# Gated MLP on one core: spatial products in blocks of four feature tiles between the two halves of each down projection

## The reference

```
z = gelu(hn @ w_in)                 # 1024 -> 4096
u, v = split(z, 2)                  # 2048 each
v = layernorm(v, g, b)
sv = W_s v + b_s                    # per block of 128 tokens and group of 256 columns; W_s is 128 x 128, masked
h = h + (u * sv) @ w_out            # 2048 -> 1024
```

## Time and profile before

| | |
|---|---|
| time, median of 3 runs | 2132.33 us (2126.59, 2132.33, 2132.35) |
| profiled execution, its own time | 2127.57 us |
| its span | 2125.8 us |
| TensorE weight loads (PEld) busy | 1689.2 us (79%) |
| VectorE (DVE) busy | 1220.3 us (57%) |
| ScalarE (ACT) busy | 756.9 us (36%) |
| GpSimd (POOL) busy | 194.0 us (9%) |

### The profile page before, as it was taken

How to read it: one execution, slowest core, us unless ns; L and a number is a source line. 1 busy time by engine, 2 the same in 40 slices (tenths; PEclk the granted TensorE clock), 3 DMA queues, 4 the chain that set the end, 5 groups by cost and what they waited for, 6 DMA issues and landing times.

```text
span 2125.8 us, 24372 instructions
## 1 busy us (share of the span) xinstructions
PE 2045.3 (96%) x10045; PEld 1689.2 (79%) x10045; DVE 1220.3 (57%) x1795; ACT 756.9 (36%) x1187; POOL 194.0 (9%) x96
## 2 busy tenths in 40 slices
PE   6999999999999999999988999999999999999998
PEld 5877876778888888799877778888877788888886
DVE  7565487747756665755565643333388676333333
ACT  4353254424433333532321432223262444232223
POOL 0000000000000000000000022222222002222221
PEclk9999999999999999999999999999999999999999
DMA  5212220211223322322311232333233113223331
GB/s 159 84 40 80 80 77 24 99 60 60 99 99 99 99 99 81 118 80 80 115 67 67 70 99 99 99 99 99 90 74 105 36 40 99 96 83 99 99 99 60
DMA packets 151375, 181.38 MB, mean 85 GB/s; under 512 B 14688, under 2 KB 120288, under 8 KB 151264
## 3 DMA queue, kind: packets, MB, share of 16 engines
q1 hardware_dynamic: 149632, 178.30, 26.0%
q10 hardware_dynamic: 1632, 1.51, 0.2%
HBM read 177.70 MB, written 2.10 MB: 85 GB/s over the span
## 4 chain that ended last, share of the span: by engine, by line
PE 86%; DVE 8%; issue 3%; ACT 3%; DMA 0%; DVEq 0%; ACTq 0%
PE bank L405 26%; PE bank L407 26%; PE bank L406 26%; PE bank L548 6%; PE bank L540 2%; DVE w_lo L826 2%; ACT w_hi L1500 1%; DVE rstd L876 1%; DVE arena L929 0%; PE bank L492 0%; DVE g_lo L840 0%; DVE arena L1409 0%; DVE arena L913 0%; DMA raw<-w_in 0%; DVE arena L932 0%
## 5 line engine op out<-in xcount | busy, mean ns | idle before, releaser
L405 PE MATMUL bank<-h_hi,w_hi 128*128 128x512 f32 x1340 | 528.5, 394 | 7.7 <-issue 4.3
L406 PE MATMUL bank<-h_lo,w_hi 128*128 128x512 f32 x1340 | 523.1, 390 | 0.0
L407 PE MATMUL bank<-h_hi,w_lo 128*128 128x512 f32 x1340 | 523.0, 390 | 0.0
L1500 ACT ACTIVATE w_hi<-raw 128x1024 fp32r<-128x1024 f32 (+2 forms) x336 | 333.7, 1037 | 501.9 <-PE bank L407 499.6
L405 PE MATMUL bank<-g_hi,w_hi 128*128 128x512 f32 (+1 forms) x1036 | 405.6, 392 | 22.8 <-DVE arena L1290 16.4
L407 PE MATMUL bank<-g_hi,w_lo 128*128 128x512 f32 (+1 forms) x1036 | 398.5, 385 | 0.0
L406 PE MATMUL bank<-g_lo,w_hi 128*128 128x512 f32 (+1 forms) x1036 | 398.1, 384 | 0.0
L884 DVE TENSOR_TENSOR resid<-bank,resid 128x512 f32<-128x512 f32 x304 | 206.4, 688 | 276.7 <-PE bank L407 276.5
L375 POOL TENSOR_TENSOR w_lo<-raw,w_hi 128x1024 fp32r<-128x1024 f32 (+1 forms) x78 | 191.2, 2452 | 1901.6 <-ACT w_hi L1500 1901.6
L826 DVE TENSOR_TENSOR w_lo<-raw,w_hi 128x1024 fp32r<-128x1024 f32 (+1 forms) x258 | 305.6, 1209 | 80.0 <-ACT w_hi L1500 78.6
L405 PEld LDWEIGHTS bank<-h_hi,w_hi 128*128 128x128 f32 x1340 | 252.5, 188 | 64.0 <-issue 11.8
(11 more groups left out here) (182 smaller groups left out, 1778.4 us busy)
## 6 DMA issues: line engine op xcount, KB each, us to landing
raw<-w SPq DMA_DIRECT2D x64, 1024.0 KB, 5.2
raw<-w_up SPq DMA_DIRECT2D x22, 1024.0 KB, 5.0
raw<-a_w_in SPq DMA_DIRECT2D x16, 1024.0 KB, 5.3
raw<-w_in SPq DMA_DIRECT2D x12, 1024.0 KB, 5.4
raw<-w_down SPq DMA_DIRECT2D x11, 1024.0 KB, 5.0
raw<-w_mkv SPq DMA_DIRECT2D x8, 1024.0 KB, 5.6
raw<-a_w_out SPq DMA_DIRECT2D x8, 1024.0 KB, 5.0
raw<-w_out SPq DMA_DIRECT2D x4, 1024.0 KB, 5.4
```

What stands on the lines that cost most here:

```text
L405: nc.tensor.matmul(dst, a_hi, b_hi, start=(k == 0), stop=False)
L406: nc.tensor.matmul(dst, a_hi, b_lo, start=False, stop=False)
L407: last = nc.tensor.matmul(dst, a_lo, b_hi, start=False, stop=(k == n - 1))
L1500: A(hi, src, ACT.Copy).then_inc(w_hi_done, 1)
```

## The change

The spatial products are made in blocks of four feature tiles, and a block stands between the two halves of a down projection. `spatial(n)` makes the four tiles of projection n. TensorE's order is now: seven up granules, `spatial(0)`, the eighth granule, then `out_half(n, 0)`, `spatial(n + 1)`, `out_half(n, 1)` for n = 0 to 3 (no spatial products in the last). Both halves finish one output tile after another. `t_four` is the memory of `t_buf` and `r_buf` in one: spatial tiles are taken into it and multiplied with u in place. The gated halves rotate: projections 0 and 3 use `g_hi` and `g_lo`, 1 and 2 the two parts of `h_hi` and `h_lo`. Four bias tiles are held at a time, two of them in the memory of the masks `causal` and `strict`.

The diff, cut to its core (the old code of the VectorE part left out):

```diff
@@ -120,9 +120,10 @@
     out += [rows("w_down", 10)]
     gate_v, gate_u = ([columns("a_w_in_2", at + COLS * c) for c in range(8)] for at in (GATE, 0))
     out += gate_v[0:6] + [("tiles", 2)] + gate_v[6:8] + [("tiles", 2)]
-    out += gate_u[0:7] + [("tiles", 2)] + gate_u[7:8]
+    out += gate_u[0:7] + [("tiles", 4)] + gate_u[7:8]
     for n in range(4):
-        out += [("tiles", 2)] * (2 if n < 3 else 1) + down("a_w_out_2", n)
+        first, second = down("a_w_out_2", n)
+        out += [first, ("tiles", 4 if n < 3 else 0), second]
     not_shared = sum(item[0] != "tiles" for item in out)
     out += mlp("w1_0", "w2_0")
     out += [columns("b_w_q_a_2", 0), columns("b_w_q_a_2", 256, n=128, tiles=1)]
@@ -188,7 +189,7 @@
         mem_k, mem_v = at(12288, KT, NMEM), at(14336, MT, D)
         mem_q = at(0, KT, S)
         prob, prob_t, keep = at(16384, 2, S), at(17408, 2, S), at(18432, 2, S)
-        t_buf, r_buf = at(19456, 2, S), at(20480, 2, S)
+        t_buf, r_buf, t_four = at(19456, 2, S), at(20480, 2, S), at(19456, 4, S)
         stick = at(20480, S + 1)
         f_z, f_a = at(12800, S), at(13312, S)
         rstd_fox, rstd_kv = at(19456, S), at(17408, S)
@@ -207,6 +208,7 @@
         one_col, b_forget = small[:, 9:10], small[:, 10:11]
         mix0_gain = small[:, 24:32]
         ln_mv, ln_std = small[:, 12:20].rearrange("p (t s) -> p t s", s=2), small[:, 20:24]
+        bias_of = [t.rearrange("p (a n) -> p a n", a=1) for t in (biases[:, 0, :], biases[:, 1, :], causal[:], strict[:])]
         ln_part = biases.rearrange("p a b -> p (a b)")[:, 0:24].rearrange("p (c s) -> p c s", s=6)
 
         bank = [ctx.enter_context(nc.psum_tensor(f"bank{i}", [P, S], F32)) for i in range(8)]
@@ -279,6 +281,8 @@
         MEM_UNITS = [(h, i) for h in range(MEM_HEADS) for i in range(TT)]
         FOX_PIECES, SB_PIECES = (4, 6, 13, 15, 21, 23, 29, 31), (4, 5, 8, 9, 12, 13, 17, 19, 31, 32)
         MEM_PIECES, MLA_PIECES = (2, 3, 13, 14, 17, 18), (5, 6, 21, 22, 29, 30)
+        GATED_HI = [g_hi[:, 0:4, :], h_hi[:, 0:4, :], h_hi[:, 4:8, :], g_hi[:, 0:4, :]]
+        GATED_LO = [g_lo[:, 0:4, :], h_lo[:, 0:4, :], h_lo[:, 4:8, :], g_lo[:, 0:4, :]]
         GROUP = {"fox": 2 * TT, "sb": 2 * TT, "mem": 2, "mla": TT}
 
         def keys(kind, i):
@@ -696,25 +700,38 @@
                 by_feature()
             by_feature()
 
-            def spatial(g):
-                for j in range(2):
+            def spatial(n):
+                for c in range(4):
                     b = next_bank()
                     for t in range(TT):
-                        c = 256 * g + P * j
-                        last = nc.tensor.matmul(b[:, P * t:P * t + P], gm_v[:, t, c:c + P], ws_t[:, g, :],
-                                                start=True, stop=True)
+                        last = nc.tensor.matmul(b[:, P * t:P * t + P], gm_v[:, t, 512 * n + P * c:512 * n + P * c + P],
+                                                ws_t[:, 2 * n + c // 2, :], start=True, stop=True)
                     full(last)
+
+            def out_half(n, half):
+
+                wait_chunk()
+                for c in range(4):
+                    dst = next_bank()
+                    for k in range(4):
+                        if half == 0 and c == 0:
+                            pe.wait_ge(g_ready, g_n.n + k + 1)
+                        last = split_sum(dst[:], w_tiles(4, slice(P * c, P * c + P), quarter_view),
+                                         [(GATED_HI[n][:, q, :], GATED_LO[n][:, q, :]) for q in range(4)],
+                                         part=range(k, k + 1))
+                    full(last)
+                if half == 0:
+                    g_n.n += 4
+                chunk.n += 1
 
             pe.wait_ge(gm_ready, 2)
             spatial(0)
             by_feature()
-            spatial(1)
             for n in range(4):
+                out_half(n, 0)
                 if n < 3:
-                    spatial(2 * n + 2)
-                down()
-                if n < 3:
-                    spatial(2 * n + 3)
+                    spatial(n + 1)
+                out_half(n, 1)
 
             def mlp():
                 by_feature(arrive=h_n.n)
@@ -1278,41 +1295,68 @@
                     V.scalar_tensor_tensor(x[:, n - 5, :], x[:, n - 5, :], gain("final_norm_g", n - 5),
                                            rstd[:, 0, :], ALU.mult, ALU.mult)
 
...
+            def spatial_biases(n):
+
+                for j in range(4):
+                    keep_order(V.scalar_tensor_tensor(bias_of[j][:, 0, :], ws_sum[:, 2 * n + j // 2, :],
+                                                      gain("a_ln_v_b_2", 4 * n + j), bs_all[:, 2 * n + j // 2, :],
+                                                      ALU.mult, ALU.add))
                 settle()
-                for j in range(2):
-                    c = 2 * g + j
+
+            def take_spatial(n):
+
+                lows_done()
+                for j in range(4):
                     take(lambda b: V.scalar_tensor_tensor(
+                        t_four[:, j, :].rearrange("p (t n) -> p t n", n=P), b[:].rearrange("p (t n) -> p t n", n=P),
+                        gain("a_ln_v_g_2", 4 * n + j), bias_of[j].to_broadcast([P, TT, P]), ALU.mult, ALU.add))
+
+            def times_u(n, j):
+                dve.wait_ge(tile_taken, spatial_end + j - 3)
+                V.tensor_tensor(t_four[:, j, :], t_four[:, j, :], gm_u[:, 4 * n + j, :], ALU.mult).then_inc(t_made, 1)
+                made.n += 1
+
+            def low_of_gated(n, j):
+                dve.wait_ge(t_made, made_end + j - 3)
+                low_half(GATED_LO[n][:, j, :], GATED_HI[n][:, j, :], t_four[:, j, :], None, g_ready)
+                g_n.n += 1
+
+            spatial_biases(0)
+            take_spatial(0)
+            spatial_end = tile.n
+            acts.n += 4
+            dve.wait_ge(act_out, acts.n)
+            for j in range(4):
+                times_u(0, j)
+            made_end = made.n
             for n in (14, 15):
                 take(scaled(gm_u[:, n, :], rstd[:, 1, :]))
+            for j in range(4):
+                low_of_gated(0, j)
             split_low()
-            for n in range(4):
-                gated(2 * n + 1)
-                gated_low(2 * n + 1)
-                if n < 3:
-                    gated(2 * n + 2)
-                    down(then=lambda: gated_low(2 * n + 2))
+            acts.n += 12
+            dve.wait_ge(act_out, acts.n)
+            for n in range(3):
+                spatial_biases(n + 1)
+                for c in range(4):
+                    back_tile(c)
+                take_spatial(n + 1)
+                spatial_end = tile.n
+                times_u(n + 1, 0)
+                times_u(n + 1, 1)
+                back_tile(4)
+                times_u(n + 1, 2)
+                times_u(n + 1, 3)
+                made_end = made.n
+                split_low()
+                back_tile(5)
+                low_of_gated(n + 1, 0)
+                low_of_gated(n + 1, 1)
+                back_tile(6)
+                low_of_gated(n + 1, 2)
+                low_of_gated(n + 1, 3)
+                back_tile(7)
+                split_low()
             down("mlp0")
 
             def mlp(following):
@@ -1750,19 +1794,25 @@
                 if n >= 2:
                     taken()
                 gelu_u(n)
-            tile.n += 2
-            hi_g(0)
+            def high_of_gated(n):
+                for c in range(4):
+                    made.n += 1
+                    act.wait_ge(t_made, made.n)
+                    high_half(GATED_HI[n][:, c, :], t_four[:, c, :])
+
+            tile.n += 4
             for n in (14, 15):
                 if n == 15:
                     split_high()
                 taken()
                 gelu_u(n)
-            for n in range(4):
-                tile.n += 2
-                hi_g(2 * n + 1)
-                if n < 3:
-                    tile.n += 2
-                    down(then=lambda: hi_g(2 * n + 2))
+            high_of_gated(0)
+            for n in range(3):
+                tile.n += 4 + 4
+                split_high()
+                high_of_gated(n + 1)
+                tile.n += 4
+                split_high()
             down(True, "mlp0")
 
             def mlp(following):
```

More of the change, by code:

```diff
@@ L1279, in _ @@
                                            rstd[:, 0, :], ALU.mult, ALU.mult)
-            def gated(g):
-                for j in range(2):
-                    c = 2 * g + j
-                    keep_order(V.scalar_tensor_tensor(biases[:, j, :], ws_sum[:, g, :], gain("a_ln_v_b_2", c),
-                                                      bs_all[:, g, :], ALU.mult, ALU.add))
+            def spatial_biases(n):
[3 more added lines that the diff above has]
+                                                      ALU.mult, ALU.add))
@@ L1287, in gated @@
                 settle()
-                for j in range(2):
```

(10 more changed lines are left out.)

## The result

The changed kernel takes **2113.09 us** in the median of 4 runs (2112.78 to 2113.93); the kernel before, with one more run, 2130.22 (2126.59 to 2132.35). The ratio is 0.9921, 95% interval 0.9907 to 0.9935: faster, by 17 us. The prediction said 2114.5, 2108 to 2124, and faster with 0.86.

A forecast was written before the change was run, and what follows sets the result against it. TensorE, busy 96% of the span, was taken as the bound, idling in the stage for VectorE's spatial take. Pauses 2.3 + 4.3, half clock 1.6 and refill 0.3 leave 8.5 us excess instead of 23.7: 2114.5 us, range 2108 to 2124.

The forecast's parts named there:

- The forecast case: Whole kernel: waits in the stage shrink to two pauses, 15.2 us saved, named time 2114.5; chance 0.81.
- matmuls of the stage by themselves: Stage's 432 large matmuls and eight blocks of 16 small ones, without waits: 111.5 us, unchanged by the edit.
- first pause, at the first take: Behind the first spatial block: TensorE waits for VectorE's weight halves, four biases and the take, 2.3 us, new.
- second pause, at the first low half: Ahead of projection 0: ScalarE's weight halves, gelu and high half, then VectorE's low half, hold TensorE 4.3 us.
- matmuls at half clock: Behind the pauses: 8 slow matmuls, 1.6 us, counted once; bounds 0 and 4.0 us.
- refill of the pipeline: TensorE refilling after three pauses: 0.3 us.
- waits in rounds 1 to 3: Down projections after the first: every wait costs nothing, covered by the second half's 48 matmuls, 10.9 us.
- excess over 111.5: Stage time beyond the matmuls' own: both pauses, half clock and refill, 8.5 us instead of 23.7.
- The margins: In each round, VectorE's first and fourth low halves are ready 2.5 and 2.0 us before TensorE wants them.
- The tile-by-tile first half: First half of each down projection, now summed tile by tile: same pace as before, nothing added.
- The named time: Whole kernel: 2114.5 us, the middle between 2112.4 from the profiled execution and 2117.1 from the median.

The follow-up runs named there:

- e6: Changed kernel with the edits of e4 and e5 together, the first weights' low halves behind the gated tiles' low halves; 2103.92 us, ratio 0.9876.
- e1: Changed kernel with each later spatial block behind both halves of a down projection, not between them; 2132.05 us, ratio to the kernel before 1.0014.
- e5: Changed kernel with the first four gated tiles' high and low halves ahead of the last two u tiles; 2108.70 us, ratio 0.9898.
- e7: Changed kernel with two more VectorE operations in each round, ahead of the weights' low halves; 2113.56 us.
- e8: Changed kernel with seven more VectorE operations in each round, ahead of the weights' low halves; 2125.92 us, ratio to the kernel before 0.9986.
- e3: Changed kernel with the first half in the old loop order, four output tiles open at once; 2113.27 us.
- e4: Changed kernel with the four biases ahead of u tile 13 and the weights' low halves behind the products with u; 2115.58 us, ratio 0.9926.
- f1: The kernel of e4 run again, unchanged, beside the changed kernel; 2111.40 us.
- e2: Changed kernel without the rotation, all four projections using g; 2118.82 us, ratio 0.9957.

## Why the prediction was right

The forecast case came true, and its terms can be checked one by one, start to start:

| term | predicted | profile after |
|---|---|---|
| matmuls of the stage by themselves | 111.5 | 112.3, the stage of e6, which has no pause |
| first pause, at the first take | 2.3 | 5.70 - 3.49 = 2.2 |
| second pause, at the first low half | 4.3 | 4.46 - 0.23 = 4.2 |
| matmuls at half clock | 8, 1.6 | 8, 1.6 |
| refill of the pipeline | 0.3 | 0.1, what is left over |
| waits in rounds 1 to 3 | 0 | 0 |
| excess over 111.5 | 8.5 | 8.9, of which 0.8 is the first row's |

The matmuls by themselves were counted 0.8 us short. A block of 32 small ones takes 3.49 us up to the next large one (1100.60 to 1104.08), not 2 x 1.70, and the step behind it is 0.32 us instead of 0.227. Both kernels have these matmuls, so the forecast saving lost little by it: 15.2 us, against 14.8 measured.

The prediction also misplaces one pause of the kernel before: the 2.71 us at 1179.33 do not stand behind the last up granule but inside the last down projection, six matmuls behind its single block of 16. No term of the sum uses the place.

- **What bounds the stage.** The take of the spatial tiles was the releaser of every idle stretch, and moving that work under matmuls took those stretches away. e1 shows that it is the place that does it.
- **The new first pause.** It was read from the instruction order alone: four tiles in a block fill the banks before VectorE is free. It is there, released by the take, as said.
- **The second pause.** ScalarE's queue (weights, gelu, then the first high half) is what it waits for; VectorE waited 2.51 us for that high half. e5, which moves the halves forward in both queues, removes the pause.
- **Nothing in the rounds.** The margins were given as 2.5 and 2.0 us; the trace has 2.5 and 2.1, and e7 and e8 bracket them from both sides.
- **The tile-by-tile first half costs nothing**, and, as e3 adds, brings nothing.
- **The clock.** Eight slow matmuls were named and eight came, but by luck. Nothing in the rows before told 8 from 14, and the same pause of 4.08 us had 14 behind it in e4 and f1. The Trainium skill (TensorE: Matmul & The Clock Gate, "Why this matters for your kernels") advises against idle gaps above a certain length between bursts of matmuls, since the clock then falls back to half rate. The traces agree for the pauses of 3.94 and 4.08 us, which all had slow matmuls behind them, and those of 1.61 and 1.97 us had none. In between the length alone did not decide: in the kernel before, 2.71 us had ten and 2.89 us none.
- **The named time.** The sum from the profiled execution gave 2112.4 and was 0.7 us off; 2114.5 had been put in the middle because the runs of before scatter between 2127 and 2132. The changed kernel's runs did not inherit that scatter. That the sum fits this well is in part luck too: from the median before over all four runs, 2130.2, it would have given 2115.0.

What I had not seen: the two pauses that I priced at 6.6 us could be removed by order alone. Both had been made by the change: the first by its larger first block, the second since the kernel before had the first high halves ahead of the last gelus.

## What to carry to other kernels

Read a wait on an evacuation as a question about order: what long stretch of matmuls needs none of the results that the busy engine is making, and could stand between the product and its use? For such a move count the whole chain to the next use (take, product, high half, low half): one buffer that is still being read keeps the last links out of the cover, as in e2, where 5.6 of 14.8 us were lost. A larger block of small products can make a wait behind it, as the first one did here (2.2 us): look at what the next user of the first bank waits for, in each queue in turn, and put the links of the chain ahead of work that nobody awaits yet.

## What the runs showed of the hardware

How long the clock stays at half after a pause did not follow from the pause's length. Behind three pauses of 1.61 us (e2) no matmul was slow; behind three of 2.47 us (e8) about 7, 2 and 8; behind three of 3.94 us (e1) about 7, 6 and 13; behind 4.08 us 8 in the changed kernel, 10 in e3, and 14 in both executions of e4. In e4 they began with the first matmul behind the pause, whose successor starts 0.56 us later; in the changed kernel two starts later:

```profile
1086.72 0.77 PE L409 MATMUL bank<-g_hi,w_hi 128*128 128x512 f32 x1 [4.08 <-DVE g_lo L857]
1087.28 0.63 PE L410 MATMUL bank<-g_lo,w_hi 128*128 128x512 f32 x1
```

So an edit that removes a pause of 2 us can be paid back in part by slow matmuls behind another one, and e4's 0.95 us is what is left of 2.2. A small gain is to be judged over several runs, or made where no other pause stands behind it, as in e6, where removing the same first pause shortened the stage by the full 2.2 us.
